# A hybrid decoder step in split fp32: the last 240 tokens' high and low source in one matmul of 480 columns

## The reference

```
x += RMSNorm(mixer(RMSNorm(x)))          # mixer: x @ w_in, attention or recurrence, @ w_out
x += RMSNorm(SwiGLU(RMSNorm(x)))         # (silu(x @ w_gate) * (x @ w_up)) @ w_down, 2816 wide inside
```

## Time and profile before

| | |
|---|---|
| runs | 1673.37, 1679.09 and 1675.85 us; median 1675.85 us |
| profiled execution, first to last instruction (span) | 1673.2 us; its granted TensorE clock is 0.969 of full speed on average |
| its own time beyond the span | not recorded apart; the median of the runs lies 2.65 us above the span |
| busy in the span | PE 1589.8 us (95%), PEld 1484.1 (89%), DVE 810.0 (48%), ACT 554.3 (33%), POOL 565.5 (34%) |

### The profile page before, as it was taken

One profiled execution on the slowest core, in us unless ns is written; L12 is line 12 of the kernel. 1 busy time (PEld: TensorE's weight loads), 2 busy tenths in 40 slices (PEclk: granted clock), 3 DMA queues, 4 the chain that ended last, 5 costly groups with the idle time before them and its releaser, 6 DMA issues. The chain is left out here.

```text
span 1673.2 us, 38351 instructions
## 1 busy us (share of the span) xinstructions
PE 1589.8 (95%) x15534; PEld 1484.1 (89%) x15534; DVE 810.0 (48%) x1353; ACT 554.3 (33%) x1051; POOL 565.5 (34%) x505
## 2 busy tenths in 40 slices
PE   7997898999899999999998999999899999999996
PEld 7997885666599999999998899999799999999995
DVE  4331126566548344443148677675448343443145
ACT  4120115556455222222245433324255222222242
POOL 0002105677524534433016234332014443433013
PEclk9999888999999999999999999999899999999998
DMA  6855988877340222223343334333140222323342
GB/s 208 315 178 180 323 308 337 285 254 257 137 176 20 96 88 88 94 98 105 104 157 113 96 89 149 102 118 87 64 139 27 88 88 89 99 92 104 105 156 86
DMA packets 87375, 238.35 MB, mean 142 GB/s; under 512 B 18333, under 2 KB 21071, under 8 KB 85793
## 3 DMA queue, kind: packets, MB, share of 16 engines
q1 hardware_dynamic: 81528, 221.41, 39.1%
q0 software_dynamic: 3392, 11.02, 1.8%
q10 hardware_dynamic: 2314, 3.96, 0.7%
HBM read 217.81 MB, written 23.77 MB: 144 GB/s over the span
## 5 line engine op out<-in xcount | busy, mean ns | idle before, releaser
L867 DVE TENSOR_TENSOR layer_w_lo<-ring,layer_w_hi 128x1024 fp32r<-128x1024 f32 (+1 forms) x136 | 223.1, 1641 | 258.4 <-ACT layer_w_hi L746 258.4
L1025 PE MATMUL layer_ps<-layer_x_hi,layer_w_hi 128*128 128x260 f32 x1312 | 268.5, 284 | 3.8 <-DVE layer_w_lo L867 2.7
L1025 PE MATMUL layer_ps<-layer_x_hi,layer_w_lo 128*128 128x260 f32 x1312 | 267.8, 284 | 0.0
L1025 PE MATMUL layer_ps<-layer_x_lo,layer_w_hi 128*128 128x260 f32 x1312 | 267.3, 283 | 0.0
L746 ACT ACTIVATE layer_w_hi<-ring 128x1024 fp32r<-128x1024 f32 (+1 forms) x136 | 158.7, 1169 | 206.8 <-PE layer_ps L1025 206.8
L1025 PE MATMUL layer_ps<-layer_h_lo,layer_w_hi 128*128 128x260 f32 x960 | 218.0, 288 | 8.6 <-DVE layer_h_lo L876 8.6
L1025 PEld LDWEIGHTS layer_ps<-layer_x_hi,layer_w_hi 128*128 128x128 f32 x1312 | 204.2, 189 | 5.3 <-DVE layer_w_lo L867 2.9
L1025 PEld LDWEIGHTS layer_ps<-layer_x_hi,layer_w_lo 128*128 128x128 f32 x1312 | 204.1, 189 | 0.0
L1025 PEld LDWEIGHTS layer_ps<-layer_x_lo,layer_w_hi 128*128 128x128 f32 x1312 | 203.5, 189 | 0.1
L1025 PE MATMUL layer_ps<-layer_h_hi,layer_w_hi 128*128 128x260 f32 x704 | 172.8, 286 | 4.9 <-DVE layer_w_lo L867 4.9
L1025 PE MATMUL layer_ps<-layer_h_hi,layer_w_lo 128*128 128x260 f32 x704 | 170.2, 282 | 0.0
(11 more groups left out here) (334 smaller groups left out, 2954.7 us busy)
## 6 DMA issues: line engine op xcount, KB each, us to landing
ring<-in_w_gu SPq DMA_DIRECT2D x88, 512.0 KB, 3.2
ring<-in_w_down SPq DMA_DIRECT2D x48, 704.0 KB, 4.1
arena<-in_cache_cmp SPq DMA_DIRECT2D x68, 256.0 KB, 6.2
ring<-in_hgrn_w_in SPq DMA_DIRECT2D x32, 512.0 KB, 3.4
ring<-in_nsa_w_in SPq DMA_DIRECT2D x21, 512.0 KB, 4.5
kv_slot<-in_slc_kv SPq DMA_DIRECT2D x32, 256.0 KB, 4.5
arena<-in_slc_kv SPq DMA_DIRECT2D x32, 256.0 KB, 4.9
X<-in_slc_kv SPq DMA_DIRECT2D x32, 256.0 KB, 4.0
```

Of the source, the lines that this page charges most:

```text
L867: dve.tensor_tensor(self.w_lo[slot][:, 0:kcs * P], c.ring[:, s, 0:kcs * P], self.w_hi[slot][:, 0:kcs * P].bitcast(F32), ALU.subtract).then ...
L1025: mm = pe.matmul(bank[:, h, 0:TH], wt[slot][:, a], xt[:, x, COLS[h]], start=start and part == 0, stop=stop and part == 2)
```

## The change

The split of the tokens moves from 260 + 260 to 280 + 240, and the tokens are laid so that they run on from one bank into the next: 280 at the end of the first bank (from column 232 on), 240 at the start of the second. The second bank then has room for two sums of 240 tokens. One matmul of 480 columns takes the hi and the lo of the last 240 tokens against the weights' hi, into two accumulators side by side; for this the hi and lo of each source lie in one buffer. A chunk is then 5 matmuls of 280, 480, 280, 280 and 240 columns, 1560 columns as before.

```diff
+FIRST = 280
+BANK_AT = 512 - FIRST
+WIDE = (FIRST, T - FIRST)
+def tokens(banks, first=0, last=T):
+    return banks.rearrange("p h n -> p (h n)")[:, BANK_AT + first:BANK_AT + last]
+COLS = [slice(0, FIRST), slice(FIRST, T)]
+def part(banks, h):
+    return tokens(banks, COLS[h].start, COLS[h].stop)
+def both_sums(banks):
+    return banks[:, 1, 0:2 * WIDE[1]]
+def merge(dve, dst, banks):
+    return dve.tensor_reduce(dst, both_sums(banks).rearrange("p (two t) -> p t two", two=2), AX, ALU.add)
+def scaled_out(dve, dst, banks, rstd, merged, n):
+    merge(dve, dst[:, COLS[1]], banks).then_inc(merged, 1)
+    dve.tensor_tensor(dst[:, COLS[0]], part(banks, 0), rstd[:, COLS[0]], ALU.mult)
+    dve.wait_ge(merged, n)
+    return dve.tensor_tensor(dst[:, COLS[1]], dst[:, COLS[1]], rstd[:, COLS[1]], ALU.mult)
+def products(pe, banks, w_hi, w_lo, x, halves, start, stop):
+    if 0 in halves:
+        pe.matmul(part(banks, 0), w_hi, x[:, 0, COLS[0]], start=start, stop=False)
+    if 1 in halves:
+        pe.matmul(both_sums(banks).rearrange("p (two t) -> p two t", two=2), w_hi, x[:, :, COLS[1]], start=start, stop=False)
+    if 0 in halves:
+        pe.matmul(part(banks, 0), w_hi, x[:, 1, COLS[0]], start=False, stop=False)
+    for h in halves:
+        mm = pe.matmul(part(banks, h), w_lo, x[:, 0, COLS[h]], start=False, stop=stop)
+    return mm
...
-        eng.tensor_tensor(pairs(dst), ps[j][:, :, 0:TH], pairs(c.rstd[:, :]), ALU.mult).then_inc(c.psum_free[j], 1)
+        scaled_out(eng, dst, ps[j], c.rstd, self.merged, n + 1).then_inc(c.psum_free[j], 1)
...
-            src, sq, y = (ps[j][:, :, 0:TH], self.mq[n % 2], pairs(Y[:, n, :])) if half is None else \
-                (ps[j][:, half, 0:TH], self.mq[n % 2][:, half, :], Y[:, n, COLS[half]])
-            act.activation(sq, src, ACT.Square).then_inc(mid.squared, 1)
-            act.activation(y, src, ACT.Copy).then_inc(self.half_out if first else c.psum_free[j], 1)
+            if half is None:
+                act.activation(Y[:, n, COLS[0]], part(ps[j], 0), ACT.Copy).then_inc(self.copied, 1)
+                act.wait_ge(self.copied, n + 1)
+            act.wait_ge(self.merged, n + 1)
+            act.sem_inc(c.psum_free[j], 1)
+            ...
+            act.activation(sq, y, ACT.Square).then_inc(mid.squared, 1)
...
+        def second_out(n):
+            self.used(dve, n)
+            merge(dve, Y[:, n, COLS[1]], self.ps[n % RING]).then_inc(self.merged, 1)
...
         for n in range(RING):
             self.used(dve, n)
+            merge(dve, Y[:, n, COLS[1]], self.ps[n]).then_inc(self.merged, 1)
             cut(n - RING, n)
...
         mid.post_mean(dve, own, 0)
+        second_out(4)
...
             mid.rest(dve, 0, k)
+            if k in (1, 4, 7):
+                second_out((k - 1) // 3 + 5)
...
+            if n in (2, 4, 6, 8):
+                down_second_out(n // 2 - 1, False)
...
+            if n in (18, 20, 22, 24):
+                down_second_out(n // 2 - 5, True)
```

More of the change, by code:

```diff
@@ L409, in one @@
                         add_squares(k - 1)
[L410 to L415, removed]
+                    a = slice(k * P, (k + 1) * P)
+                    last = products(pe, ps[j], wh[:, s % 2, a], wl[:, s % 2, a], x2[:, :, sub * kcs + k, :], (0, 1),
+                                    sub == 0 and k == 0, sub == subs - 1 and k == kcs - 1)
                     if work is not None and k == 3:
@@ L425, in token_sums @@
                 for h in range(2):
-                    mm = pe.matmul(bank[:, h, 0:TH], c.ones[:, :], squares[:, h * TH:(h + 1) * TH], start=start, stop=stop)
+                    mm = pe.matmul(part(bank, h), c.ones[:, :], squares[:, COLS[h]], start=start, stop=stop)
                 return mm
@@ L541, in sums @@
         pe.wait_ge(self.added, x + 1)
-        pe.matmul(self.bank[:, h, 0:TH], self.c.ones[:, :], self.ssq[:, COLS[h]], start=True, stop=True)\
+        pe.matmul(part(self.bank, h), self.c.ones[:, :], self.ssq[:, COLS[h]], start=True, stop=True)\
           .then_inc(self.summed, 1)
@@ L613, in gathered @@
         pe.wait_ge(self.inverse, 1)
-        pe.matmul(self.bank[:, 0, 0:TH], self.c.ones[:, :], self.ssq[:, COLS[0]], start=True, stop=True)\
+        pe.matmul(part(self.bank, 0), self.c.ones[:, :], self.ssq[:, COLS[0]], start=True, stop=True)\
           .then_inc(self.pre_summed, 1)
@@ L620, in add_squares @@
         pe.wait_ge(self.x_squared, n + 1)
[L621 removed]
+        pe.matmul(part(self.bank, h), self.c.ones[:, :], self.sq[:, n % buffers, 0:WIDE[h]], start=k == 0, stop=k == KC - 1)\
           .then_inc(self.x_added, 1)
@@ L1018, in tensor, with chunk @@
         c, ps, mid, end, done, freed = self.c, self.ps, self.mid, self.end, self.done, self.freed
-        def products(bank, slot, parts, k, x, halves, start, stop):
+        def chunk(bank, slot, x, k, halves, start, stop):
             a = slice(k * P, (k + 1) * P)
-            for part, (wt, xt) in enumerate(((self.w_hi, parts[0]), (self.w_hi, parts[1]), (self.w_lo, parts[0]))):
-                for h in halves:
-                    mm = pe.matmul(bank[:, h, 0:TH], wt[slot][:, a], xt[:, x, COLS[h]], start=start and part == 0,
-                                   stop=stop and part == 2)
-            return mm
+            return products(pe, bank, self.w_hi[slot][:, a], self.w_lo[slot][:, a], x, halves, start, stop)
         def mixer(n, halves=(0, 1)):
@@ L1061, in down @@
                     pe.wait_ge(self.used_h[x % 2], self.ROUNDS + 1)
-                mm = products(ps[u % RING], n % 2, self.hidden, k, x, halves, sub == 0 and k == 0, sub == 1 and k == SUBK - 1)
+                mm = chunk(ps[u % RING], n % 2, self.hidden[:, :, x, :], k, halves, sub == 0 and k == 0, sub == 1 and k == SUBK - 1)
                 if n == 4 * RING and k == 3:
@@ L2328, in spread_out @@
             for x in range(2):
-                for part in range(2):
-                    mm = pe.matmul((self.out_banks, self.near_banks)[h % 2][:, x, 0:TH], self.head_to[:, h, :],
-                                   self.rms_parts[part][:, COLS[x]], start=part == 0, stop=part == 1)
+                for x_part in range(2):
+                    mm = pe.matmul(part((self.out_banks, self.near_banks)[h % 2], x), self.head_to[:, h, :],
+                                   self.rms_parts[x_part][:, COLS[x]], start=x_part == 0, stop=x_part == 1)
             mm.then_inc(self.spread_in, 1)
```

101 lines of the change are left out of this document (60 added, 41 removed).

## The result

The changed kernel took 1694.31 us (median of 4 runs, 1690.3 to 1698.51) against 1674.61 (1672.65 to 1679.09): a ratio of 1.0109, with a 95% interval from 1.0081 to 1.0137. Measured once more (last experiment) it was 1.0078 (1.0059 to 1.0098). So it is slower by some 0.9%, 15 us. The sum of the prediction was 1677, no change that can be told; what came is close to the first rival (columns set the pace, 1690), and inside the range by 0.7 us at its upper end. The profiled execution has a span of 1696.6 us, 23.4 more than before.

The account below looks back on a forecast made before the run. PE's pace was taken to bound the linear layers, DVE and PE waiting in turn the crossings. Terms -17.7 + 3.7 + 9.2 + 5.5 = +0.7 us on 1673.2, plus 2.65 for the runs' median, gave 1677 us; range 1630 to 1695.

Parts of the forecast that it names:

- first rival: PE's matmuls: columns set the pace, gain only 4 us, costs of 18.4 stay, total 1690 us, slower; chance 0.20.
- PE's gain: Five matmuls a chunk instead of six: 11 ns saved on each of 1608 chunks, 17.7 us gained.
- mid crossings: Two mid crossings: later first norm, merges in DVE's queue and ACT's Squares delay the means; 4.6 us each, 9.2 lost.
- layer 1's end: End of down in layer 1: few updates behind it, so only a share of 0.2 us lost.
- layer 0's end: End crossing of layer 0: DVE without slack, merges 4 to 7 add 2.6 us; 5.5 us lost (2 to 9).
- the 715 ns: Sign in gate/up: the prediction is wrong if a chunk is under 700 or above 715 ns; 710 was forecast.
- the first reading: PE's pace: 12 ns over full speed belong to each matmul; chunk 710 ns, saves 12, taken as 11.
- second reading: PE's pace: the excess grows with columns, plus 2.4 ns a matmul; chunk 719.5 ns, saves 2.4; chance 0.20.
- third reading: PE's pace: weight loads set a 120.3 ns floor; chunk 684 ns, saves 38, 62 us gained, total 1632; chance 0.20.
- The stretch of 340 us: Gate, up and most of down, where PE alone is busy throughout: to fall from 340 us to 334.
- the clock: Longer waits in crossings may bring clock 0.50 after an idle PE: 0 to 6 us, taken as 0.
- The three instructions: Output tiles: three DVE instructions replace one, 0.8 us more a tile; mostly hidden, 3.7 us lost, of it 2 in `hgrn_in`.

Follow-up runs that it names:

- S6: The changed kernel without merges in the mixer's output alone, second accumulator unread, ACT taking the sums out of PSUM there: ratio 1.0016 to the kernel before.
- S9: The changed kernel with merges 5, 6 and 7 of the mid crossing each two steps earlier in DVE's queue: ratio 1.0070 to the kernel before.
- S5: The changed kernel with three of four merges in down's last third, and ACT's Squares, behind the next weight cut: ratio 1.0073 to the kernel before.
- S7: The changed kernel without merges in down alone, second accumulator unread there: ratio 1.0018 to the kernel before.
- S1: The changed kernel with the joint matmul of 480 columns cut into two of 240, merges kept: 1724.36 us, ratio 1.0244 to the kernel before.
- S8: The changed kernel with tokens split into 264 and 256, so the joint matmul has 512 columns: ratio 1.0072 to the kernel before.

## Why the prediction was right and wrong

**The range and the sum.** The 1694 lies in the range of 1630 to 1695, and close to its end. It does so because the range was drawn wide enough to take in the first rival; the sum that gave 1677 missed by 17 us (by the ratio of the second measurement by some 12), with PE's gain, the mid crossings and layer 1's end off the same way, and layer 0's end alone the other. The chunk, too, stayed only just below the 715 ns that the prediction named as a sign of being wrong. That much is luck.

**The step that failed: PE's gain.** "I take the first reading and 11 ns": 6.4 were measured. A joint 480 takes 218.1 ns; the first reading said 212, the second 220. The third, a floor of 120 ns by the weight load, is refuted: the 240 takes 110. Over full speed (columns/2.4) the widths 240, 256, 264, 480 and 512 have 9.7, 10.8, 11.4, 18.1 and 20.0 ns, in kernels with five matmuls: close to 0.036 ns a column and 1.6 a matmul. That is the second reading, and it speaks for a small gain. But it isn't all: six matmuls of 280 and 240 take 724 ns, six of 260 or of 264 and 256 719 to 721, where 0.453 ns a column and 1.6 a matmul make 716 of each. Something beyond the columns stands between short matmuls, 0.5 to 1.4 ns each, and more of it where the widths differ by 40. That the weight loads do it (they are then busy without a gap) was not tried. So why the pace is what it is stays open; its size is measured. (Two slips of addition in the prediction change nothing: its third reading comes to 683 ns, and costs of 27 with gains of 16 end at 1687.)

Nor was all of it realised where PE is never idle. The stretch of 340 us was to become 334 and became 1.1 us shorter. It ends at down's first mean, behind the four half tiles of the first tokens: 88 half chunks that last 387 ns (three of 280) instead of 361. That takes back some 2.3 of the 2.8 us which its 440 whole chunks save at 6.4 ns; this is an estimate from the mean paces, and it leaves 0.5 where 1.1 came.

The Trainium skill, TensorE: Matmul & The Clock Gate, section Back-to-back issue gap, has N/2.4 + 2.5 ns for an isolated matmul of N columns, which as an estimate is 202.5 for 480 columns and 102.5 for 240; the traces show 218.1 and 109.7, and they decide. Nor would a load of 111 ns hide behind 102.5, as the prediction says of the matmul of 240 columns.

**The crossings' price.** For the mid crossings 4.6 us each were forecast, 6.1 came. The stretch from mean to mean was right in kind and size (4.5): merges hold up ACT's Squares, these the cuts, and these PE (S6, S9). What the sum lacked is the part behind the second mean, 1.4 to 1.7 us. It also put the clock at nothing, because PE had worked 16.95 of 17 us; but those 17 us lie behind the second mean, and ahead of it PE already had waits. In the changed kernel they grew, the clock fell to its lower level for 10 us in each mid crossing, and at the price that S6 shows that is an estimated 1.6 us.

**The ends of down.** Layer 0: 5.5 forecast, 3.2 measured (3.8 in the last third, less 0.6 in the crossing). Layer 1: 0.2 for its whole end, 4.0 to 5.5 measured (4.6 to 6.2, less 0.6 at the end). This term was missed: I looked for updates behind the merge and not for the weight cut that stands behind it, two engines long (S5, S7).

**What was hidden.** The three instructions were priced to 0.02 us, and in gate/up they are hidden as forecast. Of the recurrence's 2 us nothing can be told: that stage took 264 to 272 us in all kernels but S1. The 2.3 us between it and the next mean were not followed up.

**Together.** PE 7 us less than forecast, layer 1's end 4 to 5 and the mid crossings 3 more, layer 0's end 2 less: that is the way from 1677 to some 1690. Attention's 6 us, which no step of mine covers, lie in the profile as well.

## What to carry to other kernels

Matmuls that are saved by widening others pay only what a matmul costs beyond its columns: measure the pace at the new width, and at the split that it needs, before counting it. A small instruction put into a queue beside a crossing costs what stands behind it on the next two engines, so look there for weight cuts and sources first, and try it behind them (in layer 1's down that gave 5 us back, in layer 0's nothing). Waits that it causes on PE can bring the clock down, which then costs again. And apply such a change only where its work is hidden: here in the input layers and gate/up, with nearly equal halves, it turned 0.9% lost into 0.35% won.

## What the runs showed of the hardware

At a granted clock of 1.00 a further column of an fp32r matmul costs 0.452 ns and not 1/2.4 = 0.417: 233.3 ns for 512 columns and 117.5 for 256 (S8), 218.1 for 480 and 109.7 for 240. Plain float32 has no such excess: in the changed kernel its instructions of 240 columns (L663) follow by 203 ns, which is 2 x 240/2.4 and 3. The order of widths matters: a 280 takes 127 ns behind a 480 and 130 to 132 behind a 240. In the changed kernel's mid crossing PE worked 2.03 of 4 us, and then the granted clock fell from 1.00 to 0.50 for 10.2 us; before the change, with PE busy for 30.79 of 31.91 us, it stayed at 1.00.
